# A hybrid decoder step whose decay exponents for two heads move from GpSimd to VectorE

## The reference, cut to what matters

```python
def gla_chunk(S, q, k, g, v):
    G = jnp.cumsum(g, axis=2)
...
    diff = G[:, :, :, None, :] - G[:, :, None, :, :]
    decay = jnp.exp(jnp.where(causal[:, :, None], diff, -jnp.inf))
    A = jnp.einsum('nhtd,nhsd,nhtsd->nhts', q, k, decay)
    o = jnp.einsum('nhts,nhsv->nhtv', A, v) + jnp.einsum('nhtd,nhdv->nhtv', q * jnp.exp(G), S)
    G_last = G[:, :, -1:, :]
    S_new = jnp.exp(G_last[:, :, 0, :])[..., None] * S + jnp.einsum('nhsd,nhsv->nhdv', k * jnp.exp(G_last - G), v)
```

## Time and profile before

| what | value |
|---|---|
| median of 3 runs | 2812.19 us (2810.12 to 2816.43) |
| time of the profiled execution | 2806.88 us |
| its span | 2805.1 us |
| TensorE busy | 2612.6 us, 93% of the span |
| VectorE busy | 1204.5 us, 43% |
| ScalarE busy | 720.0 us, 26% |
| GpSimd busy | 439.7 us, 16% |
| chain that ended last | TensorE 89%, VectorE 5%, issue 3%, ScalarE 2%, DMA 1% |

### The profile page before, as it was taken

How to read it: one execution, slowest core, us unless ns; L and a number is a source line. 1 busy time by engine, 2 the same in 40 slices (tenths; PEclk the granted TensorE clock), 3 DMA queues, 4 the chain that set the end, 5 groups by cost and what they waited for, 6 DMA issues and landing times.

```text
span 2805.1 us, 35726 instructions
## 1 busy us (share of the span) xinstructions
PE 2612.6 (93%) x12839; PEld 2151.1 (77%) x12839; DVE 1204.5 (43%) x2267; ACT 720.0 (26%) x1470; POOL 439.7 (16%) x316
## 2 busy tenths in 40 slices
PE   4998886999889999999999999999999999999997
PEld 3876755888767788788877788888877787888776
DVE  4655624344524566422224575322224764422224
ACT  2211402222222333221123333211132432211123
POOL 2421412555545102000000011000000020000000
PEclk8977988999989999999999999999999999999999
DMA  4541123666666652355555642455564622455553
GB/s 144 183 159 62 68 90 137 226 225 227 239 224 225 242 204 89 121 195 194 183 215 194 222 154 84 158 189 186 194 223 176 251 94 94 177 187 187 213 200 139
DMA packets 145204, 489.03 MB, mean 174 GB/s; under 512 B 8866, under 2 KB 79635, under 8 KB 95754
## 3 DMA queue, kind: packets, MB, share of 16 engines
q1 hardware_dynamic: 136603, 482.60, 47.9%
q10 hardware_dynamic: 8472, 4.75, 0.6%
HBM read 375.48 MB, written 112.02 MB: 174 GB/s over the span
## 4 chain that ended last, share of the span: by engine, by line
PE 89%; DVE 5%; issue 3%; ACT 2%; DMA 1%; DVEq 0%; ACTq 0%; SPq 0%
PE ps L513 26%; PE ps L515 26%; PE ps L514 26%; PE ps L700 3%; PE ps L731 2%; PE ps L548 1%; PE ps L943 1%; PE ps L942 1%; DVE x_tok L1908 1%; DMA w_both<-w_split 1%; PE ps L737 1%; DVE arena L1803 1%; PE ps L777 0%; ACT arena L1064 0%; PE ps L697 0%
## 5 line engine op out<-in xcount | busy, mean ns | idle before, releaser
L513 PE MATMUL ps<-h_hi,w_both 128*128 128x512 f32 (+2 forms) x2144 | 822.6, 384 | 11.5 <-DVE x_tok L1908 8.9
L515 PE MATMUL ps<-h_lo,w_both 128*128 128x512 f32 (+2 forms) x2144 | 813.1, 379 | 0.0
L514 PE MATMUL ps<-h_hi,w_both 128*128 128x512 f32 (+2 forms) x2144 | 810.0, 378 | 0.0
L513 PEld LDWEIGHTS ps<-h_hi,w_both 128*128 128x128 f32 x2144 | 408.3, 190 | 89.5 <-issue 13.6
L515 PEld LDWEIGHTS ps<-h_lo,w_both 128*128 128x128 f32 x2144 | 408.1, 190 | 82.8
L514 PEld LDWEIGHTS ps<-h_hi,w_both 128*128 128x128 f32 x2144 | 408.9, 191 | 79.7
L513 PE MATMUL ps<-w_both,act_hi 128*128 128x512 f32 (+1 forms) x748 | 301.1, 403 | 27.3 <-DVE act_lo L1981 27.3
L515 PE MATMUL ps<-w_both,act_hi 128*128 128x512 f32 (+1 forms) x748 | 298.5, 399 | 0.0
L514 PE MATMUL ps<-w_both,act_lo 128*128 128x512 f32 (+1 forms) x748 | 298.1, 398 | 0.0
L1981 DVE TENSOR_TENSOR act_lo<-arena,act_hi 128x512 fp32r<-128x512 f32 (+1 forms) x176 | 134.1, 766 | 341.4 <-ACT act_hi L1398 341.4
L345 POOL TENSOR_TENSOR arena<-arena 128x256 f32<-128x256 f32 x56 | 40.6, 724 | 1381.0 <-DVE arena L1803 1381.0
(11 more groups left out here) (240 smaller groups left out, 2863.0 us busy)
## 6 DMA issues: line engine op xcount, KB each, us to landing
w_both<-w_split SPq DMA_DIRECT2D x288, 1024.0 KB, 4.8
w_split<-w_both SPq DMA_DIRECT2D x96, 1024.0 KB, 6.2
w_raw<-in_w_down SPq DMA_DIRECT2D x24, 512.0 KB, 4.2
w_raw<-in_w_a SPq DMA_DIRECT2D x22, 512.0 KB, 4.2
w_raw<-in_w_b SPq DMA_DIRECT2D x22, 512.0 KB, 4.3
w_raw<-in_w_in SPq DMA_DIRECT2D x20, 512.0 KB, 4.5
x_tok<-in_x_prompt SPq DMA_DIRECT2D x16, 512.0 KB, 7.5
arena<-in_x_prompt SPq DMA_DIRECT2D x16, 512.0 KB, 6.0
```

What stands on the lines that cost most here:

```text
L513: nc.tensor.matmul(out, lhs[0], rhs[0], start=first, stop=False)
L514: nc.tensor.matmul(out, lhs[1], rhs[0], start=False, stop=False)
L515: return nc.tensor.matmul(out, lhs[0], rhs[1], start=False, stop=last)
```

## The change

For heads 2 and 3 `ahead` is taken out of GpSimd's list, in all four blocks. VectorE subtracts these exponents in the attention: in the first of a head's four chunks steps 0 and 1 before operand 0, and then always step s + 1 ahead of operand s. `exponent` and `operand` are as before. GpSimd has left only the splits of block 0, one after the other without the break at unit 20.

```diff
--- before.py
+++ after.py
@@ -492,18 +492,8 @@
                     nc.gpsimd.tensor_tensor(w_lo[:, s, :], w_raw[:, s, 0, :], w_hi[:, s, :].bitcast(F32),
                                             ALU.subtract).then_inc(w_ready, 1)
 
-            def ahead(b):
-                for h in (2, 3):
-                    for i in range(1 + LEVELS):
-                        exponent(pool, b, h, i)
-
-            for j in range(U_OUT // 4):
+            for j in range(UNITS // 4):
                 units(j)
-            ahead(0)
-            for j in range(U_OUT // 4, UNITS // 4):
-                units(j)
-            with pool.Fori(1, BLOCKS) as b:
-                ahead(b)
 
 
         @block.tensor
@@ -1856,7 +1846,11 @@
                         pool_group(b, hd, POOLED_BEHIND[i])
                     if i in AHEAD:
                         head, steps = AHEAD[i]
+                        if steps[0] == 0:
+                            exponent(dve, b, head, 0)
                         for step in steps:
+                            if step < LEVELS:
+                                exponent(dve, b, head, step + 1)
                             operand(b, head, step)
 
             def mixer_output(b, hd):
```

## The result

The changed kernel takes 2834.56 us (median of 4 runs, 2831.87 to 2836.74), against 2811.41 of the kernel before, run beside it: ratio 1.0079, interval 1.0061 to 1.0096. It is slower by 23.1 us; the forecast was 30 us slower. Behind the loops that are gone from GpSimd's list all lines of after stand 10 lower than before: 727 is the state's update (737 before), 703 the transpose, 1229 the copy of the keys, 1083 the exponential, 1792 and 1793 the products, 1831 the halves, 1841 the state, 1250 the table load. Lines 345, 346, 360, 489 and 492 keep their numbers.

The account below looks back on a forecast made before the run. TensorE, busy nearly throughout, was taken as the bound, with VectorE binding parts of block 0. 2806.88 + 12.6 (blocks 1 to 3) + 12.2 (block 0) + 5.1 (clock) = 2836.8 us profiled, 2842 as median; range 2822 to 2853.

Parts of the forecast that it names:

- The order in blocks 1 to 3: Attention of blocks 1 to 3: VectorE's late exponent delays ScalarE's key copy and TensorE; +4.2 us a block, 12.6 for three.
- The clock: Under the filler after chunk 4's wait, blocks 1 to 3: one half-clock stretch, 1.7 us a block, 5.1 in all.
- Block 0: Block 0's attention: exponents lengthen VectorE-bound chunks and GpSimd's splits block VectorE; +12.2 us, bounds 3.5 to 15.2.
- the burst of exponents: Block 0, operands of head 1: GpSimd's first burst of exponents no longer slows VectorE; -0.7 us.
- Rival A: Block 0: splits cost next to nothing, meeting waits or PSUM work; block 0 +3.5, median 2828 to 2833 us; chance 0.22.
- Rival B: TensorE's clock falls more often, after idle in block 0's VectorE-bound chunks; +5 to +12, 2847 to 2854 us; chance 0.14.
- Rival D: Whole kernel: no change that can be told, delays made up behind the attention or slack; 2807 to 2818 us; chance 0.07.
- The step to the median: Whole kernel: 5.3 us added from the profiled execution to the median of runs, 2836.8 to 2842 us.
- rival C: Chunk 5's key copy not late, GpSimd's removal wins: 0.9 us a block in chunk 2; median 2807 us; chance 0.07.

Follow-up runs that it names:

- e3: The changed kernel with VectorE's pooling group moved behind the chunk's exponents and products; 2821.45 us, ratio 1.0041 to the kernel before.
- e1: The kernel before with the change in block 0 alone, GpSimd's exponents kept in blocks 1 to 3; 2822.74 us, ratio 1.0058.
- e2: The kernel before with the change in blocks 1 to 3 alone, GpSimd's exponents kept in block 0; 2822.08 us, ratio 1.0047.
- e6: The kernel before with ScalarE's two exponentials ahead of the u tile's copy in chunks 2 and 4; 2801.19 us, ratio 0.9966.
- e7: The kernel before with exponentials ahead of the u tile's copy and VectorE's exponents two steps ahead in blocks 1 to 3; 2801.02 us, ratio 0.9965.
- e11: e7 with ScalarE's Silu table load moved from chunk 9 to behind chunk 10's copy of the keys; 2795.74 us, ratio 0.9951.
- e12: The changed kernel with GpSimd's splits from unit 20 held until block 0's keys are ready, same kernel as e4; 2828.43 us, ratio 1.0067.
- e4: The changed kernel with GpSimd's splits from unit 20 held until all keys of block 0 are ready; 2831.50 us, ratio 1.0086.
- e8: The changed kernel itself, unedited, measured again beside the kernel before; 2839.18 us, ratio 1.0101.
- e5: The changed kernel with VectorE's exponents two steps ahead of the product, exponent 3 of head 2 ahead of the pooling group; 2817.72 us, ratio 1.0038.

## Why the prediction was right, and where it was off

**The order in blocks 1 to 3: right, to its places.** Exponent 3 was to start at 1670.87, line 737 of chunk 4 to come at 1672.54. With the 15.85 us of shift these are 1686.72 and 1688.39; the rows show 1686.72 and 1688.34, 3.1 us late as computed, with the chain of three engines as described. From state 9 to 10 it was to cost 0.9 and cost 0.74; chunk 7 was to add 0.2, which is there at line 727 (the lag goes from 20.65 at state 6 to 20.85) and is gone by state 9. e3 shows the cause: the same work with the group behind it has no such wait.

**The clock: right in blocks 2 and 3.** One stretch of 3.4 us a block at the level of 1.2 GHz (1688.6 to 1692.0 at 0.50; the window shown above begins 0.2 us earlier and has 0.53), right behind the wait of 3.02 us and not behind those of 1.52 us. The lag at state 9 is 4.8 above that at state 0: 3.1 and 1.7. In block 1 the stretch began within the wait, at 1067.4, and was 6.8 us long, and the block lost 6.6. Forecast for three blocks 17.7, measured 18.7. e3 without the wait has no such stretch. Of the 6.0 us a block, 0.5 had no term: 0.15 at state 11 and 0.35 at state 14, where line 1831 comes later behind line 724 than before. The 0.35 is there in all kernels in which GpSimd makes no exponent in any block and in none of the others (e1, e2, e6, e7, e11); its cause stays open.

**Block 0: the mechanism and the terms right, 12.0 us for 12.2 by the end of chunk 10's filler.** The lag at state 15 is only 9.9, but the lag at state 0 hides what the start cost. VectorE began the operands of head 1 0.8 us earlier than before, and from there to state 0 it needed 18.81 us in place of 16.66. Before, then after:

```profile
246.95 0.43 DVE L1802 TENSOR_TENSOR arena<-arena 128x256 f32<-128x256 f32 x1 [8.73 <-ACT arena L1093]
...
263.61 0.34 DVE L1851 SCALAR_TENSOR_TENSOR state<-state,g_end,ps 128x128 f32<-128x128 f32 x1
```

```profile
246.13 0.43 DVE L1792 TENSOR_TENSOR arena<-arena 128x256 f32<-128x256 f32 x1 [8.63 <-ACT arena L1083]
...
264.94 0.34 DVE L1841 SCALAR_TENSOR_TENSOR state<-state,g_end,ps 128x128 f32<-128x128 f32 x1
```

That is 2.15 us for a forecast of 2.2. e12, with no split there, needs 15.97 (from 247.54 to 263.51), so the split took 2.84 (2.9) and the burst of exponents that is gone gave back 0.69 (0.7). From state 3 to 4 the lag grew by 3.4 us and from 7 to 8 by 3.2 (forecast 3.4), and by 0.9 to states 5 and 9 (1.0); chunks 3 to 6 together gave 5.5 for 5.3. Each instruction beside the first half of a split lost 0.83 to 0.84 us, for the 0.75 taken, and beside the second 2.03 to 2.16, for 2.15. From state 7 to the products behind chunk 10's filler it is 4.4 for 4.7. Here state 10 itself misleads: its lag falls by 7.1 us, since the splits that held VectorE there are gone, but VectorE works under the filler then, and TensorE's matmuls are not earlier for it (their lag, taken in the same way, is 11.2 us on both sides of the filler). Behind the filler 1.6 us come back by state 13. There the clock of before was down, as the same eight matmuls show, before and then after:

```profile
331.21 2.04 PE L731 MATMUL ps<-arena 128*128 128x128 f32 x8 [0.70 <-ACT arena L1183]
```

```profile
342.40 1.13 PE L721 MATMUL ps<-arena 128*128 128x128 f32 x8 [0.70 <-ACT arena L1173]
```

Before had 3.4 us at 0.50 from 331.1; after had 1.00. Rival A, harmless splits, is out: e4 and e12, without them, lose 0.4 us at each of the two places. Rival B's condition came true in block 0, its price did not. The attention there has four stretches at 0.50 in after that before has not, of 3.4, 6.8, 3.4 and 3.4 us at 282.3, 292.6, 313.0 and 323.3, and the sum above comes out with nothing for them. e1, whose block 0 has the same instructions, lacks the one of 6.8 us: its lag grows by 5.2 us from state 3 to 7, after's by 5.5, and TensorE waits 1.26 us for VectorE at 299.47, where the slower matmuls of after leave no wait. So that stretch cost 0.3 us. In e3, where three more fall in chunk 10 and behind it, block 0 lost 5.9 us more. That the forecast of 0 held was so in part luck. Rival D is out: the lag of block 3, 25.3 us at state 15, is still there at the end of the span (26.6).

**The step to the median failed.** The sum as a profiled execution was 2836.8; that execution took 2834.41. That they meet to 2.4 us is luck in part, since stretches of lower clock outside the attention, which have no term, gave back 2.5 us between blocks 2 and 3, and the same code took 2839.73 in e8. And I added 5.3 us, the distance between one profiled execution and the median before, as if it were the kernel's. It was one execution's scatter: before, the three runs of the median lie between 2810.12 and 2816.43 and the profiled one at 2806.88. The forecast of 30 us over before was missed by 7 in the first measurement (23.1) and met in e8 (29.6). What can make such differences is seen in the clock. In the trace of before there are two stretches between blocks 2 and 3 (6.8 us at 2106 and 3.4 at 2178) where after has one of 3.4 us, which gave the 2.5 us back.

**Faster (rival C)** was named with its condition, exponent 3 ready by 1667.8. It was ready at 1671.6, by the shift taken off. In e5, where VectorE starts it 0.26 us after it starts state 3, the loss is gone but for 0.4 us a block, and no 0.9 us is won either: TensorE's wait before the transpose stays 1.52 us (1.62 before), as it hangs on ScalarE's exponentials behind the u tile (e6), not on the GpSimd burst. That GpSimd slows VectorE there is true and was worth 0.1 us. The Trainium skill, "GPSIMD Engine Reference" (4.1 Engine selection), speaks for VectorE by its speed, since it has GpSimd about twice slower with two inputs. The trace has 0.42 us for half an exponent against 0.724, a ratio of 1.7, and the ratio decided nothing.

## What to carry to other kernels

Before moving work to a faster engine, write down where in that engine's list it will stand and who waits for its result, and follow that chain over all engines; here a thing worth 0.67 us cost 3.1 because 3 us of other work stood ahead of it, and the half clock behind the wait made it 4.8. Give what is moved the slack that it had (here: two steps ahead, not one), and look for the same fault in the neighbouring lists: the order on ScalarE was worth 3.7 us a block, with or without the change. And look at what the engine left behind does earlier once its list is shorter: its weight splits came into the one stretch that VectorE bounds.

## What the runs showed of the hardware

A GpSimd instruction with one input holds VectorE as well as one with two: instructions of 0.42 us took 1.25 and 1.26 beside the TENSOR_SCALAR of 1.31 and 1.23 us, and ended 0.27 us behind it. They lose what is left of it when they start. In blocks 2 and 3 the wait of 3.02 us on TensorE was followed by a stretch of 3.4 us at 1.2 GHz, and e8, e4, e12 and e2 repeat the lag that goes with it (4.4 us from state 4 to 5) to 0.1 us; waits of 1.5 to 1.6 us in the same chunks were not followed by one. Stretches of lower clock elsewhere wander: two traces of one kernel stood 6 us apart before the code in question began, and its ratio came out at 1.0079 and 1.0101, so effects of 0.1% are read from distances inside the trace and not from medians, and inside a trace only where no such stretch lies in one kernel and not in the other: the same code of block 0 lost 8.6 us in one trace and 14.5 in another.
